# A fused encoder block: group norm's scale and bias in VectorE's two steps, and one group of Gram heads ahead of the gate product

## The reference, cut to what matters

```python
y_f, k_f = rwkv7_direction(r, k, v, kk, wd_f, ad_f, ..., False)
y_b, k_b = rwkv7_direction(r, k, v, kk, wd_b, ad_b, ..., True)
y = y_f + y_b
mean = jnp.mean(y, axis=-1, keepdims=True)
var = jnp.mean(jnp.square(y - mean), axis=-1, keepdims=True)
y = ((y - mean) * lax.rsqrt(var + GN_EPS)).reshape(B, T, RWKV_DIM)
y = y * ln_x_gain + ln_x_bias
bonus = jnp.sum(heads(r) * k_bonus * r_k_h, axis=-1, keepdims=True) * heads(v)
g = jax.nn.sigmoid(gd) @ g_up
return (y + bonus.reshape(B, T, RWKV_DIM)) * g
```

## Time and profile before

| | |
|---|---|
| median of three runs | 1914.92 us (1914.83 to 1915.35) |
| the profiled execution | 1915.28 us, its span 1913.5 us |
| granted TensorE clock, mean | 0.998 |
| TensorE matmul busy | 1883.2 us (98% of the span), 11523 matmuls |
| VectorE, ScalarE, GpSimd busy | 1359.4 (71%), 981.1 (51%), 374.7 us (20%) |
| DMA | 147 GB/s over the span |

### The profile page before, as it was taken

One profiled execution on the slowest core, in us unless ns is written; L12 is line 12 of the kernel. 1 busy time (PEld: TensorE's weight loads), 2 busy tenths in 40 slices (PEclk: granted clock), 3 DMA queues, 4 the chain that ended last, 5 costly groups with the idle time before them and its releaser, 6 DMA issues.

```text
span 1913.5 us, 34042 instructions
## 1 busy us (share of the span) xinstructions
PE 1883.2 (98%) x11523; PEld 1656.3 (87%) x11523; DVE 1359.4 (71%) x2443; ACT 981.1 (51%) x1811; POOL 374.7 (20%) x470
## 2 busy tenths in 40 slices
PE   7999999999999999999999999999999999999997
PEld 6888889999999999999999887888888888888886
DVE  5777656888888888888888956856555555656565
ACT  5666544555555555555555545534444444444343
POOL 2000000544444444444444421000000000000001
PEclk9999999999999999999999999999999999999999
DMA  8555766433333333333332247566656565666663
GB/s 239 149 142 148 193 187 172 120 93 94 95 95 95 95 95 95 94 90 90 88 89 94 88 148 226 163 194 193 189 194 188 194 187 191 196 187 186 196 189 118
DMA packets 415370, 281.25 MB, mean 147 GB/s; under 512 B 14074, under 2 KB 372700, under 8 KB 414556
## 3 DMA queue, kind: packets, MB, share of 16 engines
q1 hardware_dynamic: 414560, 277.43, 49.9%
q10 hardware_dynamic: 764, 3.21, 0.4%
HBM read 278.52 MB, written 2.10 MB: 147 GB/s over the span
## 4 chain that ended last, share of the span: by engine, by line
PE 95%; DVE 2%; issue 1%; ACT 0%; POOL 0%; DMA 0%; SPq 0%; DVEq 0%; POOLq 0%; ACTq 0%
PE bank L1785 19%; PE bank L1956 13%; PE bank L1789 10%; PE bank L1958 6%; PE bank L1803 6%; PE bank L1804 6%; PE bank L1805 6%; PE bank L2045 3%; PE bank L2089 2%; PE bank L2107 2%; PE bank L2112 2%; PE bank L1935 1%; PE bank L2174 1%; PE bank L2153 1%; PE bank L1937 1%; PE bank L1936 1%
## 5 line engine op out<-in xcount | busy, mean ns | idle before, releaser
L1785 PE MATMUL bank<-xT,whi 128*128 128x512 f32 x1664 | 418.2, 396 | 0.2 <-DVE xT L1010 0.2
L1785 PEld LDWEIGHTS bank<-xT,whi 128*128 128x128 f32 x1664 | 303.4, 188 | 56.5 <-DVE xT L1010 0.4
L1956 PE MATMUL bank<-xT,whi 128*128 128x512 f32 x1024 | 312.9, 413 | 0.1
L1573 DVE TENSOR_TENSOR wlo<-raw,whi 128x1024 fp32r<-128x1024 f32 x126 | 154.4, 1226 | 162.5 <-ACT whi L919 158.2
L919 ACT ACTIVATE whi<-raw 128x1024 fp32r<-128x1024 f32 x126 | 133.2, 1058 | 205.5 <-PE bank L1805 205.5
L1789 PEld LDWEIGHTS bank<-xT,wlo 128*128 128x128 f32 x1664 | 222.7, 191 | 14.5
L1789 PE MATMUL bank<-xT,wlo 128*128 128x256 f32 x1664 | 226.9, 282 | 0.0
L960 DVE TENSOR_TENSOR wlo<-raw,whi 128x1024 fp32r<-128x1024 f32 (+1 forms) x119 | 183.5, 1543 | 45.2 <-ACT whi L467 41.1
L459 ACT ACTIVATE whi<-raw 128x1024 fp32r<-128x1024 f32 x192 | 200.9, 1047 | 0.0
L1803 PE MATMUL bank<-whi,ft 128*128 128x512 f32 x512 | 199.3, 389 | 0.0
L1804 PE MATMUL bank<-wlo,ft 128*128 128x512 f32 x512 | 199.3, 389 | 0.0
(11 more groups left out here) (267 smaller groups left out, 3493.1 us busy)
## 6 DMA issues: line engine op xcount, KB each, us to landing
raw<-in_w_in SPq DMA_DIRECT2D x106, 1024.0 KB, 5.9
raw<-in_w_ffn_up SPq DMA_DIRECT2D x64, 1024.0 KB, 6.4
raw<-in_w_ffn_down SPq DMA_DIRECT2D x64, 1024.0 KB, 5.0
raw<-in_w_out SPq DMA_DIRECT2D x16, 1024.0 KB, 5.3
raw<-in_w_in SPq DMA_DIRECT2D x4, 768.0 KB, 4.8
xtok<-in_x SPq DMA_DIRECT2D x2, 1024.0 KB, 6.0
upg<-in_g_up SPq DMA_DIRECT2D x16, 128.0 KB, 2.2
hres<-in_x ACTq DMA_DIRECT2D x1, 2048.0 KB, 10.7
```

The costliest lines, as they stand in the source:

```text
L1573: V.tensor_tensor(wlo[:, u % 2, 0:1024], raw[:, (u + 2) % 4, 0:1024], whi[:, u % 2, 0:1024].bitcast(f32), ALU.subtract)
L1785: M(bank[:, :], hi[:, P * k:P * k + P], xT[:, k, :, :], start=k == 0, stop=False)
L1956: M(bank[:, :], hi[:, P * k:P * k + P], xT[:, k, :, :], start=k == 0, stop=False)
```

## The change

Two edits. ScalarE's step L835 goes, and with it the semaphore y2. VectorE's scale becomes one scalar_tensor_tensor, y times gain times the spread rstd, and its add_bonus another, y plus bias plus bonus. The column of the gain and of the bias is picked by a register in the loop. Second, on TensorE `heads(2)` of the next pair moves from behind the gate product to ahead of it; heads(3) stays behind it.

```diff
--- before.py
+++ after.py
@@ -285,7 +285,7 @@
             khs=2, kbs=1, t2=2, vtp=1, vts=1, gram=4, gmask=8, dt0=2, d0p=2, d0=2, ctm=12, wmm=12, wev=12,
             ddm=10, dtm=12, tse=10, dup=10, dtup=12, kbtp=1, kbs2=1, rhsm=2, rhsc=2, um=2, ue=2, resm=2, rese=2, dum=2, due=2,
             smm=1, sme=1, ym=1, ye=1, gy=1, ysqs=1, var=1, vars=1, vpow=1, vrep=1, vbc=1, bonm=1, bonv=1, asc=1, plc=1,
-            y1=1, y2=1, y3=1, y4=1, y5=1,
+            y1=1, y3=1, y4=1, y5=1,
 
             mg_hi=1, mg_lo=1, mg_last=1, x_free=1, part=1, p_ev=1, p_add=1, o_pl=1, o_cp=1, ld_h=1, ld_g=1, m_h=1,
             xs=1, h_tp=1, h_hi=1, h_lo=1, up_re=8, up_ad=8, up_sq=8, up_hi=8, up_lo=8, dn_acc=4, f_g=1, f_last=1, f_o=1, ld_g2=1, done=1,
@@ -831,9 +831,6 @@
                 spread(i)
                 if n is not None:
                     plain(n, 0)
-                w("y1")
-                A.activation(yc[:], yc[:], ACT.Identity, scale=pB[:, bass.ds(48 + i, 1)],
-                             bias=pB[:, bass.ds(64 + i, 1)]).then_inc(s["y2"].sem, 1)
 
             for j in range(3):
                 dense(j, 0)
@@ -1304,13 +1301,13 @@
                     w = self.w
                     w("vbc")
                     w("ye")
-                    inc(V.tensor_tensor(yc[:], ysb[:], PB[7][:, 0:T], ALU.mult), "y1")
+                    inc(V.scalar_tensor_tensor(yc[:], ysb[:], self.col(pB, 48), PB[7][:, 0:T], ALU.mult, ALU.mult), "y1")
 
                 def add_bonus(self):
                     w = self.w
-                    w("y2")
+                    w("y1")
                     w("bonv")
-                    inc(V.tensor_tensor(yc[:], yc[:], bon[:], ALU.add), "y3")
+                    inc(V.scalar_tensor_tensor(yc[:], yc[:], self.col(pB, 64), bon[:], ALU.add, ALU.add), "y3")
 
                 def gate(self):
                     w = self.w
@@ -2229,8 +2226,8 @@
                     x = M(PB[7][:, 2 * tb:2 * tb + 2], ysq[:, P * tb:P * tb + P], hsel, start=True, stop=True)
                 inc(x, "var")
                 if gram:
+                    gram.heads(2)
                     gram.gate()
-                    gram.heads(2)
                     gram.heads(3)
                     gram.bonus()
                     dense(2, d2, 0, EARLY)
```

## The result

The changed kernel takes 1921.08 us, median of 8 runs (1920.19 to 1921.79), against 1915.15 us for the kernel before in the same comparison (8 runs, 1914.56 to 1916.05). The ratio is 1.0029, with a 95% interval of 1.002 to 1.0038: slower, by 5.9 us, where 3.6 was forecast. Put on the 1914.92 us from which the forecast started, the ratio gives 1920.5 us. That is above the forecast's own range (1917.6 to 1919.4) and inside the range for 8 in 10, which ends at 1920.8; the 1921.08 taken by itself lies just beyond it.

What follows compares the result with a forecast made beforehand. TensorE, gapless, was taken to bound the kernel: the new order adds 6.37 us (fourteen bodies 5.74, pair 14 0.63), the l=2 stall returns 2.73, so 3.64 slower, 1918.5 us; own range 1917.6 to 1919.4, 8 in 10 1915.4 to 1920.8.

Steps and rivals of the forecast that it cites:

- body 14: Loop pair i=14, where keep(1) ends later: bonus was to start 0.63 us later, against 0.41 in the other bodies.
- The split of the 0.41: TensorE, delay of bonus per body: 0.20 us new exit and entry, 0.20 later start of heads(2), 0.01 rounding and dearer second start.
- Rival 1: TensorE: switching between 64- and 128-partition products is free, only the wait for keep(1) costs; 1915.6 us, chance 0.13.
- rival 3: TensorE: stopping for keep(1) costs more than a crossing, small gate products come slower, 0.1 per pair; 1920.0 us, chance 0.08.
- the wait at l=2: TensorE, step l=2 at body start, waits for VectorE's late `Dm` update: 0.21 us lost in thirteen bodies, 2.73 us to come back.
- I take 0.47 and 0.57 with 0.14 between them: VectorE's tail: assumed us for new scale and new add_bonus, and the gap between; add_bonus would end at 751.93, not 752.50.
- The tail had 0.75 in hand: VectorE: slack, in us, by which the tail could run later and the `Dm` update still start by 754.16.
- the deadline: Latest start of VectorE's `Dm` update, 754.16, for TensorE to start step l=2 unhindered at 754.66.
- rival 2: VectorE: two new steps cost over 1.8 us together beside GpSimd, so the l=2 loss stays; 1921.3 us at 2.0, chance 0.14.
- the 947 ns of L1253: VectorE: dearest two-input operation of this size in the trace, taken as upper bound for each new step.

Runs made afterwards that it cites:

- e7: Kernel before, with bonus moved between heads(2) and heads(3), one more crossing between 128 and 64 partitions without a new binding wait: 1919.49 us, one run.
- e2: Kernel after with the old order on TensorE, so the VectorE and ScalarE part alone: 1912.59 us against 1915.45, ratio 0.9985.
- e4: Kernel after with the old TensorE order, scale and add_bonus writing PSUM bank 7 in place, gate step reading it there: 1912.19 us against 1915.45, ratio 0.9983.
- e6: e4 with the new TensorE order, heads(2) ahead of the gate product: 1919.18 us against 1915.61, ratio 1.0019.
- e1: Kernel before with only the TensorE order changed, heads(2) ahead of the gate product: 1920.71 us against 1915.45, ratio 1.0028.
- e3: Kernel after with add_bonus as a plain addition of two tiles, the bias left out: 1918.75 us, one run.
- e8: Kernel before with both heads(2) and heads(3) ahead of the gate product: 1932.81 us, one run.

## Why the prediction went as it did

**Right: what bounds the kernel, and each piece on TensorE.** Every tenth on TensorE's row was paid. Expected from var to bonus 3.68, measured 3.70; heads(2) 0.05 behind keep(1), the gate product 1.06 behind it, heads(3) 0.90 behind that, all as written (1.07 and 0.90 in the rows above). From var to bonus body 14 was to cost 0.63 and cost 0.62, and by the length of the body 0.59. Timeline of VectorE and TensorE in that body, after:

```profile
1092.98 0.72 DVE L1270 COPY_PREDICATED G<-cst,bank 128x512 f32<-128x512 int32 x1
...
1093.75 0.70 PE L2042 MATMUL bank<-AR,ta 64*128 64x256 f32 x4 [0.37 <-DVE G L1270]
...
1094.81 0.38 PE L2017 MATMUL bank<-gah,ugh 128*128 128x256 f32 x1
...
1095.71 0.70 PE L2042 MATMUL bank<-AR,ta 64*128 64x256 f32 x4
...
1096.77 0.39 PE L2050 MATMUL bank<-rkp,halves 128*128 128x256 f32 x1
```

The split of the 0.41 into 0.20 for the crossing and 0.20 for the later start needs a word, though its sum was right. If heads behind var pay the same 0.10 for the entry as behind bonus in e7, a crossing takes 0.30 of it and the wait for keep(1) only 0.12; no run has heads behind var without that wait. The fourth tenth of e7 isn't paid anew here, since the second gate product is as late behind var (0.21) as behind heads (0.22). Rival 1, free crossings, falls with e7, and rival 3, a dearer stop, with the gate product and heads(3) at their normal distances.

**Right: the wait at l=2 and its cure.** The stop exists, it comes from the tail, and where the tail is early or unhindered it goes entirely (e2, e4, e6). It was slightly larger than I took it: e4 shows 0.86 for the stretch without any wait, so 0.23 was lost and not 0.21. E2 got back 3.0 us in the loop, 2.73 were forecast.

**Wrong in size: the price of the tail.** The step that failed is "I take 0.47 and 0.57 with 0.14 between them", and with it the unspoken term that the gate step would keep its 0.44. The 0.47 and the 0.14 held (0.48 and 0.15). Add_bonus measured 0.97, and the gate step 0.78, so add_bonus and gate step together took 0.74 more than reckoned. Scale also starts 5.28 from var where I gave 5.13; in e1, where it is a plain product behind the same `vbc`, it starts at 5.16, so most of that is its register instruction. That makes 0.89 in all. The 0.57 itself was no price of the step either, but 0.42 and a meeting with GpSimd. The tail had 0.75 in hand by my count, and misses the deadline by 0.14. The distances at l=2 say the same, 0.13, by the distances from the last filler product before to the next one behind (means of 0.972 before, 0.875 after, 0.740 in e4, all start to start of single instructions). Per body 0.43 is lost on TensorE (the first product behind bonus starts 3.616 from var before, 4.043 after) and 0.10 comes back, which makes the 0.34 net in place of 0.20, to a hundredth. That is what separates 3.6 from 5.3.

The mechanism is rival 2's, a tail that is dearer than assumed and a deadline missed from some point on, with about half of its price, though not by its condition: the two new steps cost 1.45 together, not over 1.8. That the time lies inside the wide range at all is luck: the range left rival 2 out, and its mechanism at half its price happens to end beside rival 3's 1920.0. I had priced that rival from the 947 ns of L1253 in the earlier trace rows and discounted it because both new steps would have to cost as much. It needed only one of them, and a third step that the change doesn't touch. Why the 947 was there, in an operation whose like takes 0.42 elsewhere, was the question to ask. The answer was in the profile of the kernel before, in GpSimd's rows of the same timeline, which I hadn't laid beside VectorE's:

```profile
737.15 0.80 POOL L1684 TENSOR_TENSOR rk<-rk,nb 128x256 f32<-128x256 f32 x1
737.27 0.95 DVE L1253 TENSOR_TENSOR kh<-kh,dec 128x256 f32<-128x256 f32 x1
...
738.90 0.80 POOL L1726 TENSOR_TENSOR gt<-gt,gup 128x256 f32<-128x256 f32 x1
739.03 0.95 DVE L1253 TENSOR_TENSOR kh<-kh,dec 128x256 f32<-128x256 f32 x1
```

Both instances start behind a GpSimd step and end 0.27 and 0.28 behind its end, and so do all but one of the 32 (that one, at 0.83, starts behind a cast on GpSimd). The 947 ns was a meeting, not a price.

**Shown by the runs:** the two engines exclude each other in these steps. Four things carry it. One instruction takes 0.53 (e2) or 0.97 (after) by whether it starts 0.20 ahead of GpSimd's or together with it. In the first case GpSimd's takes 0.88 instead of 0.68. With one input in PSUM (e6), at the same moment, both take what they take alone. And with no GpSimd step beside it (pair i=15 of the kernel after) the instruction takes 0.48. The Trainium skill (SBUF — State Buffer, Who interferes with whom) has the rule: a VectorE instruction with two SBUF inputs contends with a GpSimd instruction that reads SBUF, and the one that issues second blocks until the first is done. The trace agrees on the cure, and on who pays wherever the two starts lie apart; in the kernel after they are recorded 0.01 apart, VectorE's first, and it is VectorE that is held. It differs in the amount: the blocked VectorE step ends 0.28 us behind GpSimd's end, though on its own it takes 0.42 or more.

**Two parts that don't add.** The order alone costs 5.25 in the loop and the other part gives 3.03; together that would be 2.2, and it is 5.3. The order moves the tail's steps and GpSimd's against each other, and so undoes what the other part gives. The reckoning moved TensorE's products, the deadline and the tail, but left GpSimd's steps out of it.

**What is left.** The part on VectorE and ScalarE in the old order beats both kernels, by 0.15% (e2, interval of the ratio 0.9976 to 0.9994), and with PSUM operands by 0.17% (e4, 0.9974 to 0.9992); which of the two is better the runs don't tell. No experiment took GpSimd's step away inside the loop; the 0.48 of pair i=15 stands for it.

## What to carry to other kernels

Where one engine has no gaps, as TensorE here, a new order on it is paid in full, and its price could be read from the trace to a few hundredths. What couldn't be read off is a duration on VectorE beside a busy GpSimd: before you assume one, lay the rows of VectorE and GpSimd beside each other at the new times, count the inputs that lie in SBUF, and see who starts first. If a step then lies badly, moving one operand to PSUM is a surer cure than shifting it by a tenth.

## What the runs showed of the hardware that was not expected

- VectorE and GpSimd, each with two inputs of 128x256 f32 in SBUF: the VectorE step that comes with or behind GpSimd's ends 0.28 us behind it (before, after and e1 alike, the merge in e2, e3 and e6, and L1253 before); a GpSimd step that starts 0.13 or 0.20 behind VectorE's takes 0.87 to 0.88 instead of 0.68 (e3, e2). With one VectorE input in PSUM, 0.49 and 0.68 (e6).
- A switch on TensorE from products of 128 partitions to products of 64 and back costs 0.41 us (e7): 0.10 before the first, 0.10 in the first half-group, 0.10 on leaving, and 0.10 between the first and the second product behind.
- An instruction on VectorE that takes a column at a place held in a register and waits for the one before it starts 0.15 us behind that one; the plain form in its place 0.03 (after and e3). Where it had nothing to wait for, no hole was seen: scale starts 5.08 from var in e2 as in the kernel before.
- A stop of TensorE right ahead of the hardware loop's jump made the first product behind the jump 0.36 us later than the stop alone (e8; 0.39 in the loop against 0.03 in pair i=15).
